# First block's feed-forward: gate and up projections by seven half products, in three up/down phases

## What is computed

```python
def swiglu(x, w13, w2):
    a, b = jnp.split(x @ w13, 2, axis=-1)
    return (jax.nn.silu(a) * b) @ w2
...
        x = layer_norm(ALPHA * x + mix, ln_g[layer, 0], ln_b[layer, 0])
        x = layer_norm(ALPHA * x + swiglu(x, ffn_w13[layer], ffn_w2[layer]), ln_g[layer, 1], ln_b[layer, 1])
```

## Time and profile before

| | |
|---|---|
| median of 3 runs | 3571.84 us (3570.96 to 3572.84) |
| the profiled execution | 3576.24 us |
| its span, first to last instruction | 3574.5 us |
| granted PE clock, mean share of full speed | 0.995 |
| the two `ffn_stage` calls, from the span's start | about 386 to 754 us and 1014 to 1382 us |

### The profile page before, as it was taken

How to read it: one execution, slowest core, us unless ns; L and a number is a source line. 1 busy time by engine, 2 the same in 40 slices (tenths; PEclk the granted TensorE clock), 3 DMA queues, 4 the chain that set the end, 5 groups by cost and what they waited for, 6 DMA issues and landing times. The chain is left out here.

```text
span 3574.5 us, 41808 instructions
## 1 busy us (share of the span) xinstructions
PE 3495.8 (98%) x15772; PEld 2779.2 (78%) x15772; DVE 1580.9 (44%) x2147; ACT 1299.0 (36%) x1826; POOL 466.8 (13%) x382
## 2 busy tenths in 40 slices
PE   9999999999999999999999999999999999999998
PEld 7787788877778886888886688887888886688886
DVE  3386433355643334333266733325333266733325
ACT  4243422234542224332344533325332344533224
POOL 0000111000211100221001022102221001022102
PEclk9999999999999999999999999999999999999999
DMA  4200233322023331333220233313333220133322
GB/s 146 88 1 30 82 95 101 105 71 77 27 80 99 102 99 62 99 94 109 83 78 19 65 94 100 111 61 99 94 97 109 82 84 19 53 97 97 112 71 77
DMA packets 78029, 292.06 MB, mean 82 GB/s; under 512 B 8656, under 2 KB 11472, under 8 KB 77648
## 3 DMA queue, kind: packets, MB, share of 16 engines
q1 hardware_dynamic: 77328, 289.31, 25.4%
q10 hardware_dynamic: 576, 1.05, 0.1%
HBM read 288.22 MB, written 2.10 MB: 81 GB/s over the span
## 5 line engine op out<-in xcount | busy, mean ns | idle before, releaser
L157 DVE TENSOR_TENSOR w_low<-w_raw,w_high 128x1024 fp32r<-128x1024 f32 (+4 forms) x513 | 672.5, 1311 | 1513.6 <-ACT w_high L152 1513.5
L191 PE MATMUL bank<-x_high,w_high 128*128 128x512 f32 x2856 | 1118.7, 392 | 19.2 <-DVE w_low L157 9.7
L193 PE MATMUL bank<-x_high,w_low 128*128 128x512 f32 x2856 | 1111.6, 389 | 0.0
L192 PE MATMUL bank<-x_low,w_high 128*128 128x512 f32 x2856 | 1111.5, 389 | 0.0
L152 ACT CAST w_high<-w_raw 128x1024 fp32r<-128x1024 f32 (+4 forms) x513 | 555.1, 1082 | 834.2 <-PE bank L193 824.1
L191 PEld LDWEIGHTS bank<-x_high,w_high 128*128 128x128 f32 x2856 | 536.2, 188 | 145.2 <-DVE w_low L157 14.8
L193 PEld LDWEIGHTS bank<-x_high,w_low 128*128 128x128 f32 x2856 | 536.2, 188 | 111.8
L192 PEld LDWEIGHTS bank<-x_low,w_high 128*128 128x128 f32 x2856 | 536.2, 188 | 111.0 <-issue 1.7
L191 PE MATMUL bank<-hidden_high,w_high 128*128 128x512 f32 x1056 | 410.8, 389 | 0.0
L192 PE MATMUL bank<-hidden_low,w_high 128*128 128x512 f32 x1056 | 410.8, 389 | 0.0
L193 PE MATMUL bank<-hidden_high,w_low 128*128 128x512 f32 x1056 | 410.8, 389 | 0.0
(11 more groups left out here) (567 smaller groups left out, 3511.3 us busy)
## 6 DMA issues: line engine op xcount, KB each, us to landing
w_raw<-in_stream SPq DMA_DIRECT2D x381, 512.0 KB, 3.5
w_raw<-in_stream SPq DMA_DIRECT2D x96, 704.0 KB, 4.0
...
out<-result SPq DMA_DIRECT2D x4, 512.0 KB, 2.7
...
```

Of the source, the lines that this page charges most:

```text
L157: self.nc.vector.tensor_tensor(self.lo[:, j % 2, 0:size], self.raw[:, j % RAW_SLOTS, 0:size], self.hi[:, j % 2, 0:size].bitcast(F32), ALU. ...
L191: nc.tensor.matmul(out, lhs[0], rhs[0], start=start, stop=False)
L192: nc.tensor.matmul(out, lhs[0], rhs[1], start=False, stop=False)
L193: return nc.tensor.matmul(out, lhs[1], rhs[0], start=False, stop=stop)
```

## The change

The stage takes two tiles of output features at a time. The weights of such a pair, 256 features by 1024, are cut into 2 x 2 blocks (two tiles, two halves of the 1024 inputs), and so is x (two halves of the features, two halves of the 512 tokens). Instead of the eight block products the code forms seven, named A11, A12, S2, S1, S3, A22 and S4 after their weight blocks or sums of blocks (A1j and A2j are the first and second tile's halves; S1 to S4 are sums and differences of them). Each is 4 x 3 matmuls with 256 token columns. Three of them run on sums of blocks of x, made once at the stage's start (`t_high`, `t_low`; A22's operand is a sum, too, written over half of x_high).

In detail:

- 11 groups of two tiles; the first group (4 jobs) stays classical. The other ten make 20 pairs n = 0 to 19, a gate pair (n even) and an up pair (n odd) in turn.
- Per pair, ACT casts 7 parts of 512 columns (`part`), DVE makes 4 sums (`summed`) and 7 low parts, ACT copies the bank Y three times (`copy` 1 after A11, 2 after S2, 3 after S3) into SBUF, and DVE joins copies with the banks X and Z (`join`) into quarters of the output named 11, 22 and 12; quarter 21 stays in bank Y. Silu runs on quarters of the gate, products on quarters of the up (`multiply`). The parts of pair n+1 are made while PE multiplies pair n; products A22 and S4 of pair n run within pair n+1.
- Three phases: groups 0 to 3, 4 to 7, 8 to 10. After each comes a down projection over the hidden tiles of that phase (8, 8 and 6 tiles, 8 jobs each), added to the residual; hidden buffers hold 8 tiles. The products A22 and S4 of a phase's last pair stand between the first pieces of down jobs 0 and 1.
- The stage's lists are written out in full, without loops. The host packs the same weights in the new order.

The core of the diff (the body's indentation is cut by 16 columns):

```diff
+PHASES = ((0, 4), (4, 8), (8, 11))
 RAW_SLOTS = 4
 SPLIT_SLOTS = 2
...
+class Seven:
+    SLOT = {"A11": 0, "A12": 1, "S2": 2, "S1": 3, "S3": 4, "A22": 5, "S4": 6}
...
+        self.first = [2 * (a - skip) if a > skip else 0 for a, _ in PHASES]
+        self.last = [2 * (b - skip) - 1 for _, b in PHASES]
...
+        self.hi = ctx.enter_context(sbuf(nc, "part_high", [P, 7, T], F32R))
+        self.lo = ctx.enter_context(sbuf(nc, "part_low", [P, 7, T], F32R))
+        self.sums = ctx.enter_context(sbuf(nc, "part_sums", [P, 3, T], F32))
+        self.tail = W.raw[:, 0:4, 2 * T:2 * T + self.HALF]
...
             @block.sync
             def _(sp):
-W.fetch(sp, S, jobs)
...
+    for n in range(V.first[f], V.last[f] + 1):
+        sp.wait_ge(S.part_sums, V.summed("S4", n))
+        sp.wait_ge(S.part_low, V.made("A12", n))
+        refill(V.job(n, 0))
+        sp.wait_ge(S.part_low, V.made("A22", n))
+        refill(V.job(n, 1))
+    for d in range(DT):
+        sp.wait_ge(S.low_ready, ahead + classic + DT * f + d + 1)
+        refill(down_at[f] + d)
             @block.tensor
             def _(pe):
...
     for q in range(DT):
-        mm = three(nc, C.bank[u][:, :], W.parts(0, u, q * P),
-                   (C.xhi[:, q, :], C.xlo[:, q, :]), q == 0, q == DT - 1)
+        mm = classical(c, q)
...
-repeat(pe, up_jobs, up, head=1)
...
+def product(n, kind, to, start, stop):
...
+    for q in range(4):
+        at = slice(q * P, (q + 1) * P)
+        x = operand(kind, q)
+        nc.tensor.matmul(bank(n, to), V.hi[:, s, at], x[0], start=start and q == 0, stop=False,
...
+        nc.tensor.matmul(bank(n, to), V.hi[:, s, at], x[1], start=False, stop=False,
...
+        mm = nc.tensor.matmul(bank(n, to), V.lo[:, s, at], x[0], start=False,
+                              stop=stop and q == 3, skip_group_check=True)
+    mm.then_inc(S.part_done, 1)
...
+for f in range(len(PHASES)):
+    a, b = V.first[f], V.last[f]
+    for n in range(a, b + 1):
+        if n >= 2:
...
+            pe.wait_ge(S.joined, V.joined("12", n - 2))
...
+        product(n, "A11", "Y", True, False)
+        product(n, "A12", "X", True, True)
+        if n > a:
+            a22(n - 1)
+        pe.wait_ge(S.copied, V.copied(1, n))
+        if n == 0:
+            pe.wait_ge(S.t_low, 3)
+        product(n, "S2", "Y", False, False)
+        if n > a:
+            s4(n - 1)
+        product(n, "S1", "Z", True, False)
+        pe.wait_ge(S.copied, V.copied(2, n))
+        product(n, "S3", "Y", False, False)
+    tiles = 2 * (PHASES[f][1] - PHASES[f][0])
+    c = classic + DT * f
+    pe.wait_ge(S.low_ready, ahead + c + 1)
+    pe.wait_ge(S.residual_done, 1 + DT * f)
+    pe.wait_ge(S.hid_low, 2 * PHASES[f][1])
+    down(f, 0, 0, tiles - 2)
+    a22(b)
+    s4(b)
+    pe.wait_ge(S.low_ready, ahead + c + 2)
+    pe.wait_ge(S.residual_done, 2 + DT * f)
+    down(f, 1, 0, tiles - 2)
+    pe.wait_ge(S.hid_low, 2 + 2 * PHASES[f][1])
+    down(f, 0, tiles - 2, tiles)
+    down(f, 1, tiles - 2, tiles)
+    for d in range(2, DT):
+        pe.wait_ge(S.low_ready, ahead + c + d + 1)
+        pe.wait_ge(S.residual_done, 1 + DT * f + d)
+        down(f, d, 0, tiles)
...
             @block.scalar
             def _(act):
...
+def part(kind, n):
+    if n:
+        act.wait_ge(S.part_done, V.done(kind, n - 1))
+    if kind[0] == "S":
+        act.wait_ge(S.part_sums, V.summed(kind, n))
...
+        act.wait_ge(*V.arrival(n, int(kind[1])))
+    nc.scalar.copy(V.shaped(kind, V.hi[:, V.SLOT[kind], :]),
...
+def copy(i, n):
+    act.wait_ge(S.part_done, V.done({1: "A11", 2: "S2", 3: "S3"}[i], n))
+    if i == 1 and n:
+        act.wait_ge(S.joined, V.joined("11", n - 1))
+    elif i == 2 and n >= 2:
+        act.wait_ge(S.joined, V.joined("12", n - 2))
+    elif i == 3 and n:
+        act.wait_ge(S.joined, V.joined("22", n - 1))
+    nc.scalar.copy(copy_of(i, n), bank(n, "Y")).then_inc(S.copied, 1)
+
+def silu(q, n):
...
+    else:
+        act.wait_ge(S.joined, V.joined(q, n))
+        src = gated[:, t, c]
+    nc.scalar.activation(gated[:, t, c], src, ACT.Silu).then_inc(S.quarter_gated, 1)
+def hidden_high(f, n, t):
+    act.wait_ge(S.quarter_hid, V.quarter("21" if t else "12", n))
...
+high(2, 2)
+high(3, 3)
+part("A11", 0)
+part("A12", 0)
+for i, (t, src) in enumerate(((0, t_a), (2, t_b), (1, t_a))):
+    act.wait_ge(S.t_sums, i + 1)
+    t_part(thi[:, t, :, :], src)
+    if i < 2:
...
+        nc.scalar.activation(gated[:, i, :], C.bank[i][:, :], ACT.Silu).then_inc(S.gate_ready, 1)
+for kind in ("S2", "S1", "S3"):
+    part(kind, 0)
+for t in range(2):
+    act.wait_ge(S.hid_ready, t + 3)
+    nc.scalar.copy(hhi[:, t, :], hidden[:, t, :]).then_inc(S.hid_high, 1)
...
+for half in range(2):
+    t_part(C.xhi[:, 2 * half:2 * half + 2, late], t_c[half])
+for f in range(len(PHASES)):
+    a, b = V.first[f], V.last[f]
+    for n in range(a, b + 1):
+        up = n % 2
+        if n > a:
+            copy(3, n - 1)
+        copy(1, n)
+        if n < b:
+            part("A11", n + 1)
+        else:
+            high(classic + DT * f, down_at[f])
+        if n > a and up:
+            silu("22", n - 1)
+        if n < b:
+            part("A12", n + 1)
+        if not up:
+            silu("11", n)
+        part("A22", n)
+        if n > a:
+            if up:
+                silu("21", n - 1)
+            else:
+                hidden_high(f, n - 1, 1)
+        copy(2, n)
+        if n < b:
+            part("S2", n + 1)
+        else:
+            high(classic + DT * f + 1, down_at[f] + 1)
+        part("S4", n)
+        if n > a and up:
+            silu("12", n - 1)
+        if n < b:
+            part("S1", n + 1)
+        if n > a and not up:
+            hidden_high(f, n - 1, 0)
+        if n < b:
+            part("S3", n + 1)
+    copy(3, b)
+    hidden_high(f, b, 1)
+    hidden_high(f, b, 0)
+    final = f == len(PHASES) - 1
+    for d in range(DT):
+        if d + 2 < DT or final and d + 2 == DT:
+            high(classic + DT * f + d + 2, down_at[f] + d + 2)
+        if d == DT - 3 and not final:
+            for kind in ("A11", "A12", "S2", "S1", "S3"):
+                part(kind, b + 1)
...
             @block.vector
             def _(dve):
...
+def part(kind, n):
+    dve.wait_ge(S.part_high, V.made(kind, n))
...
+def summed(kind, n):
+    if n:
+        dve.wait_ge(S.part_low, V.made(kind, n - 1))
+        dve.wait_ge(S.part_sums, V.summed("S4", n - 1))
+    if kind == "S1":
...
+        x, y, op = V.raw(n, 2, 1), V.raw(n, 2, 2), ALU.add
+    elif kind == "S2":
+        dve.wait_ge(S.part_sums, V.summed("S1", n))
+        x, y, op = V.source("S1", n), V.raw(n, 1, 1), ALU.subtract
...
+        x, y, op = V.raw(n, 1, 1), V.raw(n, 2, 1), ALU.subtract
...
+        dve.wait_ge(S.part_sums, V.summed("S2", n))
...
+def join(q, n):
+    t, c = V.at(q)
+    i, kind = {"11": (1, "X"), "22": (3, "Z"), "12": (2, "Z")}[q]
+    dve.wait_ge(S.copied, V.copied(i, n))
+    dve.wait_ge(S.part_done, V.done({"11": "A12", "22": "S1", "12": "S4"}[q], n))
+    dst = (hidden if n % 2 else gated)[:, t, c]
...
+    nc.vector.tensor_tensor(dst, copy_of(i, n), bank(n, kind), ALU.add).then_inc(S.joined, 1)
+def multiply(q, n):
+    t, c = V.at(q)
+    dve.wait_ge(S.quarter_gated, V.quarter(q, n))
+    if q == "21":
...
+low(2, 2)
+nc.vector.tensor_tensor(t_a, b12, b11, ALU.subtract).then_inc(S.t_sums, 1)
+low(3, 3)
+nc.vector.tensor_tensor(t_b, b22, b12, ALU.subtract).then_inc(S.t_sums, 1)
+part("A11", 0)
+part("A12", 0)
+t_low(tlo[:, 0, :, :], t_a, thi[:, 0, :, :], 1)
...
+nc.vector.tensor_tensor(t_a, t_b, b11, ALU.add).then_inc(S.t_sums, 1)
+t_low(tlo[:, 2, :, :], t_b, thi[:, 2, :, :], 2)
...
+    at = slice(2 * half, 2 * half + 2)
+    nc.vector.tensor_tensor(t_c[half], C.h[:, 4 + 2 * half:6 + 2 * half, early], t_a[:, at, :],
+                            ALU.subtract).then_inc(S.t_sums, 1)
+t_low(tlo[:, 1, :, :], t_a, thi[:, 1, :, :], 3)
+dve.wait_ge(S.t_low, 3)
+summed("S1", 0)
+summed("S2", 0)
+summed("S3", 0)
+part("S2", 0)
+summed("S4", 0)
+part("S1", 0)
+part("S3", 0)
+for t in range(2):
+    dve.wait_ge(S.multiplied, ahead + t + 5)
+    dve.wait_ge(S.gate_ready, t + 3)
+    nc.vector.tensor_tensor(hidden[:, t, :], C.bank[4 + t][:, :], gated[:, t, :],
+                            ALU.mult).then_inc(S.hid_ready, 1)
...
+    t_low(C.xlo[:, at, late], t_c[half], C.xhi[:, at, late], 4 + half)
...
+for f in range(len(PHASES)):
+    a, b = V.first[f], V.last[f]
+    for n in range(a, b + 1):
+        up = n % 2
+        if n < b:
+            summed("S1", n + 1)
+            summed("S2", n + 1)
+        if n > a:
+            join("22", n - 1)
+        if n < b:
+            part("A11", n + 1)
+            part("A12", n + 1)
+        if n > a and not up:
+            multiply("22", n - 1)
+        join("11", n)
+        if n == b:
+            low(classic + DT * f, down_at[f])
+        part("A22", n)
+        if n > a and not up:
+            multiply("21", n - 1)
+        if up:
```

(32 more changed lines are left out.)

356 lines of the change are left out of this document (265 added, 91 removed).

## The result

The changed kernel takes **3604.1 us** (median of 4 runs, 3603.53 to 3605.42), the kernel before 3571.4 us (4 runs, 3570.24 to 3572.84): a ratio of 1.0092, 95% interval 1.0074 to 1.0109, 32.7 us slower. Forecast were 3597, in 3566 to 3616.

The account below looks back on a forecast made before the run. The prediction took DVE and ACT waiting on each other, not PE, to pace the changed kernel. Phases +1.9, down projection +4.4 and start +6.3 made 12.6 us a stage, 25.2 in both: 3597 us, range 3566 to 3616.

Parts of the forecast that it names:

- the ring of DVE and ACT: Middle of a phase: DVE and ACT wait on each other, 22.9 us per two pairs; PE needs 20.16; chance 0.64.
- The five waits: Middle of a phase: DVE reaches five low parts before ACT has made their high parts, 5.0 us per two pairs.
- POOL: Middle of a phase: POOL's two low parts of hidden tiles slow DVE beside them, 0.87 us per two pairs.
- Rival 2: POOL's operations cost DVE 1.12 us each, 1.4 more per two pairs, +19 us, 3616 us; chance 0.09.
- The phases: Three phases of six, eight and six pairs take 219.7 us against 217.8, +1.9 us a stage.
- PE's wait at a gate pair: Middle of a phase: PE waits for join 12 at a gate pair's first product, 0.5 us.
- The down parts: Down projection in three: PE waits for third jobs' weights and the last hidden tile, +4.4 us a stage.
- The third job's wait: Down projection: job 2's weights need job 0's slot, so PE waits 1.3 us, 1.35 in the third phase.
- The last hidden tile of the third phase: Down projection of the third phase: this tile comes 0.45 us late for PE.
- The start: Stage's start: DVE's list delays ACT's copies; PE waits 4.5 us at S2, 2.7 at S3; +6.3 us a stage.
- Rival 3: Middle of a phase: PE's 1.9 us waits drop its clock to 1.2 GHz; +10, 3607, at worst 3621 us; chance 0.07.
- Rival 4: PE's 256-wide matmuls with fresh weights run slower than 0.120 us; at 0.13, 3597 us; chance 0.02.

## Why the prediction was right, and where it was off

- **The main step holds**: the ring of DVE and ACT, not PE, paces the middle. The five waits measured 4.86 for 5.0, and taking their causes away, in ACT's list alone, gave 28 us.
- **POOL** was put at 0.87 a ring and is 1.10 by the rows, 1.09 by the run without it. Rival 2 in full (2.24) is not what happened, for the reason given: DVE idles in part of each POOL operation. That was a property of the waits, and ended with them.
- **The phases** were put at +1.9 a stage and are +4.9 (2.8 in the second, 1.1 in the third, and in the first, without its start, taken to be as much as in the third). The step that is mis-sized is the ring, 0.36 short (DVE's own work 0.3, POOL 0.23, the waits 0.13 too long), which comes up to three times a phase, and PE's wait at a gate pair, 0.5 forecast, 0.95 measured (1.07 from the start of the matmul ahead, less 0.12). The band's "0.4 us on a ring is 7 us" is 5.6 by the seven rings a stage that rival 2 counts.
- **The down parts**: +4.4 forecast, +5.3 measured. The third job's wait of 1.3 is there (1.25 over the pitch of 0.23). The last hidden tile of the third phase is 0.86 late, not 0.45. The four waits make 4.5 of it; the rest is not attributed.
- **The start**: +6.3 forecast, 7.6 measured in the first stage, 7.0 in the second. Wait S2 4.27 for 4.5; S3 0.72 for 2.7, because S2 and S1 ran at 1.2 GHz in between, which the forecast did not see and which cost nothing: the start of S3 is set by copy 2. The 0.6 that the classical jobs were to gain came in part, as PE's wait at the third fell from 1.00 to 0.55, but not in their length (25.0 and 24.3 us in the two stages, 24.4 and 24.3 before).
- **Rival 3**: the clock didn't fall in the middle (granted 1.00 from us 528 to 616, with six waits of up to 1.7 us in them). TensorE: Matmul & The Clock Gate of the Trainium skill (A second HAM failure mode: psum-queue depth-cycling) tells of a kernel in which frequent short idles made the clock swing; six waits of 0.4 to 1.7 us, 11 to 12 us apart, did not do it here. **Rival 4** is out: 0.120 us a matmul in the second phase of every kernel that forms the seven products.
- The sum came out 7.5 short of the medians' 32.7: 5.2 and 4.6 in the two stages, less 2.3 that the rest of the program became shorter against the medians.
